# Query and key preparation inside the projections, and V multiplied with tokens on partitions

## The reference

```python
# even layer: part of the combined projection is attention with grouped heads
q, k, v = split(h @ w_in)            # 8 query heads, 2 key/value heads of 64
q, k = rms_norm(q, q_gain), rms_norm(k, k_gain)      # per head and token
ql, kl = apply_axial_rope(ql, cos, sin), apply_axial_rope(kl, cos, sin)   # latent tokens only
p = softmax(q . k * 64 ** -0.5); out = p @ v

# odd layer: differential attention, no norm of q and k
pl = hl @ w_in                       # q, k, v of 1024 columns each; q for latent tokens only
ql, kl = rope(ql), rope(kl)
p = softmax(q1 . k1 / 8) - lam * softmax(q2 . k2 / 8); out = p @ v
```

## Time and profile before

| what | value |
|---|---|
| time, median of 3 runs | 5691.41 us (5691.09 to 5696.93) |
| the profiled execution | 5694.67 us, its span 5692.4 us |
| PE busy | 4159.3 us, 73% |
| DVE busy | 2207.1 us, 39% |
| ACT busy | 1421.9 us, 25% |
| POOL busy | 638.5 us, 11% |

### The profile page before, as it was taken

The page is one execution under the profiler, slowest core; times in us unless marked ns, Lnnn a source line. Parts: engine busy times, 40 slices in busy tenths (PEclk is TensorE's granted clock), DMA queues, the critical chain, the costliest instruction groups (busy, mean ns, idle before and its releaser), DMA issues. The chain is left out here.

```text
span 5692.4 us, 71074 instructions
## 1 busy us (share of the span) xinstructions
PE 4159.3 (73%) x23474; PEld 2745.7 (48%) x23475; DVE 2207.1 (39%) x4258; ACT 1421.9 (25%) x3188; POOL 638.5 (11%) x1135
## 2 busy tenths in 40 slices
PE   5597499396794949756499994599189955499983
PEld 0386277285683848635133331488056644133321
DVE  0312644565656656543300002411767743300003
ACT  0211255343333424312011110210056632011111
POOL 0000100131322313310200002000300000100001
PEclk9798799698897979877699997699599977799996
DMA  9421100101001010034468897321520023357996
GB/s 334 150 88 66 71 10 8 41 1 25 10 1 34 1 34 1 25 122 141 179 253 307 353 398 294 134 83 66 190 78 10 10 87 122 156 221 316 396 427 232
DMA packets 210800, 778.83 MB, mean 137 GB/s; under 512 B 52000, under 2 KB 95285, under 8 KB 185957
## 3 DMA queue, kind: packets, MB, share of 16 engines
q1 hardware_dynamic: 158376, 624.64, 29.0%
q10 hardware_dynamic: 37696, 103.04, 4.7%
q0 software_dynamic: 14544, 48.79, 2.3%
HBM read 656.45 MB, written 122.58 MB: 137 GB/s over the span
## 5 line engine op out<-in xcount | busy, mean ns | idle before, releaser
L2305 PE MATMUL ex_bY<-ex_w,ex_aT 128*64 x880 | 390.9, 597 | 74.6 <-DVE ex_aT L2368 65.5
L2305 PE MATMUL ex_bG<-ex_w,ex_xT 128*64 x880 | 405.6, 616 | 41.0 <-SPq L2226 27.5
L2308 PE MATMUL ex_bG<-ex_w,ex_xT 128*64 128x512 f32 x880 | 405.6, 616 | 0.0
L367 PE MATMUL p_acc<-hT,p_wh 128*128 128x512 f32 (+1 forms) x1056 | 376.0, 356 | 24.7 <-DVE p_wl L379 24.7
L2308 PE MATMUL ex_bY<-ex_w,ex_aT 128*64 128x512 f32 x880 | 391.1, 597 | 0.0
L2305 PE MATMUL ex_bU<-ex_w,ex_xT 128*64 x880 | 386.6, 592 | 0.0
L2308 PE MATMUL ex_bU<-ex_w,ex_xT 128*64 128x512 f32 x880 | 386.6, 592 | 0.0
L367 PE MATMUL p_acc<-hT_rest,p_wh 128*128 128x512 f32 (+1 forms) x1056 | 375.8, 356 | 0.0
L367 PE MATMUL p_acc<-hT,p_wl 128*128 128x512 f32 (+1 forms) x1056 | 375.1, 355 | 0.0
L2366 DVE TENSOR_TENSOR ex_a<-ex_sg,ex_bU 128x512 f32<-128x512 f32 x55 | 37.8, 687 | 811.2 <-PE ex_bU L2308 811.2
L703 PE MATMUL ad_S<-ad_K,ad_q 64*128 64x512 f32 (+1 forms) x768 | 191.4, 577 | 125.7 <-DMA ad_lqk<-in_od_lk 120.6
(11 more groups left out here) (361 smaller groups left out, 8861.7 us busy)
## 6 DMA issues: line engine op xcount, KB each, us to landing
ex_w<-in_moe_w_gate SPq DMA_DIRECT2D x64, 2048.0 KB, 12.0
ex_w<-in_moe_w_up SPq DMA_DIRECT2D x64, 2048.0 KB, 16.0
ex_w<-in_moe_w_down SPq DMA_DIRECT2D x64, 2048.0 KB, 14.3
mods_w<-in_mod_w SPq DMA_DIRECT2D x24, 2048.0 KB, 13.1
projT_dram<-p_o ACTq DMA_DIRECT2D x44, 640.0 KB, 2.9
yb_dram<-ex_y ACTq DMA_DIRECT2D x55, 512.0 KB, 10.1
p_w<-in_od_w_in SPq DMA_DIRECT2D x12, 1024.0 KB, 5.1
n_x<-x_dram SPq DMA_DIRECT2D x20, 512.0 KB, 3.8
```

What stands on the lines that cost most here:

```text
L367: mm = nc.tensor.matmul(acc[u % 2][c][:, 0:n], a[:, u // 2, k, at], b[:, k, t0:t0 + n], start=k == 0 and x == 0, stop=k == KT - 1 and x == 2)
L2305: nc.tensor.matmul(bank[0:BR, :], stationary[:, k, 0:BR], w[:, ds(slot0 + (offset + k * n), 512)], start=k == 0, stop=k == tiles - 1)
L2308: m = nc.tensor.matmul(bank[BR:P, :], stationary[:, k, BR:P], w[:, at:at + 512], start=k == 0, stop=k == tiles - 1)
```

## The change

Both `qk_phase` stages are removed. The two projections get functions of their own.

In `even_proj_phase` tiles 0 to 3 are q, tile 4 is k, tile 5 is V and tiles 6 to 19 go to `projT` as before. For a q tile ACT squares the evacuated `o` and writes gain times `o` to `xn`; DVE and POOL rotate `xn`, and ACT stores it to `qT`. The sums of squares come from 10 matmuls of 2 columns, issued after chunk 0 of the next tile; their root and reciprocal (20 numbers per partition) are kept in `rq`. They are not applied to q: the first attention multiplies each row of scores by `rq` where it multiplied by 1.0. The k tile is normed in full, with the matmul against `blockones` after each chunk of tile 5, the long reciprocal, gain, rotation and store. Tile 5 (V) is transposed after the chunks of tile 6 and copied by ACT.

In `odd_proj_phase` q is computed for the 1024 latent tokens only (two chunks of 512) and rotated in `o`; k is rotated in `o` too. V is computed with tokens on partitions: for each 256 columns, 10 token tiles of 24 matmuls of 256 columns, evacuated by DVE and ACT in turn and stored to `v_dram`. The second attention loads V from there (10 loads of 512 KB, after the first K and q) and waits for all of it before its first product with V.

The diff, cut to its core:

```diff
-def proj_phase(nc, sems, tag, w_dram, hT, outT):
...
+def even_proj_phase(nc, sems, d, hT, projT, qT, kT, V, rq):
...
+    NQ, KEYS, VALS, PLAIN = AW // P, AW // P, AW // P + 1, A_COLS // P
...
+                def extras(g, c):
+                    if c == 0 and 1 <= g <= NQ:
+                        if g == 1:
+                            pe.wait_ge(const_in, C_IN)
+                        else:
+                            pe.wait_ge(sd_done, g - 1)
+                        pe.wait_ge(sq_done, g)
+                        for t in range(NT):
+                            x = nc.tensor.matmul(sums[:, 2 * t:2 * t + 2], sq[:, t * P:(t + 1) * P], hc[:, :], start=True, stop=True)
+                        x.then_inc(ss_done, 1)
+                    if g == KEYS + 1:
+                        pe.wait_ge(sq_done, NQ + 1)
+                        pe.wait_ge(sd_done, NQ + c)
+                        t0, n = TCH[c]
+                        nc.tensor.matmul(sums[:, 0:n], ones[:, :], sq[:, t0:t0 + n], start=True, stop=True).then_inc(ss_done, 1)
+                    if g == VALS + 1:
+                        pe.wait_ge(dve_ev, 4 + 2 * VALS + 2)
+                        pe.wait_ge(act_ev, 2 + VALS + 1)
+                        if c:
+                            pe.wait_ge(v_done, c)
+                        for t in range(4 * c, min(4 * c + 4, NT)):
+                            x = nc.tensor.transpose(tr[:, (t - 4 * c) * P:(t - 4 * c + 1) * P], o[:, VALS % 2, t * P:(t + 1) * P], ident[:, :])
+                        x.then_inc(tr_done, 1)
...
+                            extras(tile(i, u), c)
...
+                def rope(g):
+                    if g == 0:
+                        dve.wait_ge(const_in, C_IN)
+                    else:
+                        dve.wait_ge(rope_done, g)
+                    x = xn[:, g % 2, CTX:TOK]
+                    nc.vector.tensor_tensor(ra[:, :], x, cos[:, :], ALU.mult).then_inc(ra_done, 1)
+                    nc.vector.stream_shuffle(sh[:, :], x, SWAP16).then_inc(sh_done, 1)
+                    dve.wait_ge(ra_done, g + 1)
+                    dve.wait_ge(rb_done, g + 1)
+                    nc.vector.tensor_tensor(x, ra[:, :], sh[:, :], ALU.add).then_inc(rope_done, 1)
+                def queries(g):
+                    if g < NQ:
+                        dve.wait_ge(gained, g + 1)
+                        rope(g)
+                    if 1 <= g <= NQ:
+                        dve.wait_ge(sd_done, g)
+                        nc.vector.reciprocal(rq[:, :, 2 * (g - 1):2 * g], sd[:, :, :]).then_inc(rq_done, 1)
+                def keys():
+                    dve.wait_ge(sd_done, NQ + 3)
+                    nc.vector.reciprocal(rk[:, :], rk[:, :]).then_inc(kn_done, 1)
+                    dve.wait_ge(kn_done, 1)
+                    dve.wait_ge(x_out[KEYS % 2], 16 * (KEYS // 2))
+                    nc.vector.scalar_tensor_tensor(out=xn[:, KEYS % 2, :], in0=o[:, KEYS % 2, :], scalar=gain[:, 1:2], in1=rk[:, :], op0=ALU.mult, op1=ALU.mult).then_inc(kn_done, 1)
+                    dve.wait_ge(kn_done, 2)
+                    dve.sem_inc(o_out[KEYS % 2], 16)
+                    rope(KEYS)
...
+                def squares(g):
+                    if g:
+                        act.wait_ge(ss_done, g)
+                    nc.scalar.activation(sq[:, :], o[:, g % 2, :], ACT.Square).then_inc(sq_done, 1)
+                    if g < NQ:
+                        if g == 0:
+                            act.wait_ge(const_in, C_IN)
+                        if g >= 2:
+                            act.wait_ge(x_out[g % 2], 16 * (g // 2))
+                        nc.scalar.activation(xn[:, g % 2, :], o[:, g % 2, :], ACT.Copy, scale=gain[:, 0:1]).then_inc(gained, 1)
+                        act.wait_ge(sq_done, g + 1)
+                        act.wait_ge(gained, g + 1)
+                        act.sem_inc(o_out[g % 2], 16)
...
+                def query_sums(g):
+                    act.wait_ge(ss_done, g)
+                    if g >= 2:
+                        act.wait_ge(rq_done, g - 1)
+                    nc.scalar.activation(sd[:, :, :].rearrange("p t h -> p (t h)"), sums[:, 0:2 * NT], ACT.Sqrt, scale=1.0, bias=eps[:, 0:1]).then_inc(sd_done, 1)
...
+                        if g == VALS + 1:
+                            for c in range(NB):
+                                values(c)
+                            act.wait_ge(v_done, NB)
+                            act.sem_inc(o_out[VALS % 2], 16)
...
+                        if g <= KEYS:
+                            squares(g)
+                        if g >= PLAIN:
+                            act.dma_start(projT[ds(i * (U * P) + u * P, P), :], o[:, u % 2, :]).then_inc(o_out[u % 2], 16)
+                        if 1 <= g <= KEYS:
+                            store(g - 1)
+                        if g == VALS + 1:
+                            store(KEYS)
...
-def qk_phase(nc, sems, tag, d, projT, tiles, vrows, V, gains=None):
...
+def odd_proj_phase(nc, sems, d, hT, qT, kT, v_rows):
...
+    QCH = ((CTX, 512), (CTX + 512, 512))
+    NQ, NK = U * QI, U * (KI - QI)
...
+                with pe.Fori(0, QI) as i:
+                    tiles(i, QCH, lambda g: g + 1)
+                with pe.Fori(QI, KI) as i:
+                    tiles(i, TCH, lambda g: 2 * g - NQ + 1)
+                for i in range(KI, ITERS):
+                    for v in range(2):
+                        pe.wait_ge(rest_done, 2 * i + v + 1)
+                        for t in range(NT):
+                            n = 2 * NT * (i - KI) + NT * v + t
+                            if t % 2 == 0:
+                                pe.wait_ge(dve_ev, V_DVE + n // 2)
+                            if t % 2 == 1 or n == 0:
+                                pe.wait_ge(act_ev, V_ACT + n // 2)
+                            for k in range(KT):
+                                for x, (a, b) in enumerate(((lead, wh), (rest, wh), (lead, wl))):
+                                    mm = nc.tensor.matmul(acc[t % 2][0][:, 0:2 * P], a[:, k, t * P:(t + 1) * P], b[:, v, k, :],
+                                                          start=k == 0 and x == 0, stop=k == KT - 1 and x == 2)
+                            mm.then_inc(mm_done, 1)
...
+                def rope(i, u, evacuated):
+                    g = U * i + u
+                    x = o[:, u % 2, CTX:TOK]
+                    dve.wait_ge(dve_ev, evacuated)
+                    dve.wait_ge(act_ev, 2 + g + 1)
+                    nc.vector.tensor_tensor(ra[:, :], x, cos[:, :], ALU.mult).then_inc(ra_done, 1)
+                    nc.vector.stream_shuffle(sh[:, :], x, SWAP16).then_inc(sh_done, 1)
+                    dve.wait_ge(ra_done, g + 1)
+                    dve.wait_ge(rb_done, g + 1)
+                    nc.vector.tensor_tensor(x, ra[:, :], sh[:, :], ALU.add).then_inc(rope_done, 1)
+                    dve.wait_ge(rope_done, g + 1)
...
+                def queries(i):
+                    for u in range(U):
+                        dve.wait_ge(o_out[u % 2], 16 * (2 * i + u // 2 + 1))
+                        dve.wait_ge(mm_done, q_seen(i, u, 0))
+                        t0, n = QCH[0]
+                        nc.vector.tensor_scalar(o[:, u % 2, t0:t0 + n], acc[u % 2][0][:, 0:n], HD ** -0.5, None, ALU.mult).then_inc(dve_ev, 1)
+                        if u % 2 == 1:
+                            split(i + 1, u // 2)
+                        rope(i, u, 2 + U * i + u + 1)
...
+                def tiles(i, chunk, seen, last, scale, store):
+                    for u in range(U):
+                        act.wait_ge(o_out[u % 2], 16 * (2 * i + u // 2 + 1))
+                        t0, n = chunk
+                        act.wait_ge(mm_done, seen(i, u, 1))
+                        nc.scalar.activation(o[:, u % 2, t0:t0 + n], acc[u % 2][1][:, 0:n], ACT.Copy, scale=scale).then_inc(act_ev, 1)
+                        if u % 2 == 1:
+                            act.wait_ge(mm_done, seen(i, u, last))
+                            split(i + 1, u // 2)
+                        act.wait_ge(rope_done, U * i + u + 1)
+                        store(i, u)
...
+                            act.dma_start(v_rows[2 * a * P:(2 * a + 2) * P, c0:c0 + 2 * P].rearrange("(t p) c -> p t c", p=P), vo[:, e % 2, :, :]).then_inc(v_out[e % 2], 16)
...
-def gqa_qk(nc, sems, d, projT, qT, kT, V):
...
+                    if i == 0 and v_rows is not None:
+                        for t in range(NT):
+                            sp.dma_start(V[:, t, :], v_rows[t * P:(t + 1) * P, :]).then_inc(v_in, 16)
...
+                    if i == 0 and m == 0 and v_rows is not None:
+                        pe.wait_ge(v_in, 16 * NT)
...
-                        nc.vector.tensor_scalar(p[:, u, c, a:a + w], S[j % 2][c][:, 0:w], 1.0, None, ALU.mult, ALU.max, accum_out=top[:, u, c, i:i + 1]).then_inc(s_out, 1)
+                        pair, t, nk = units[n]
```

(75 more changed lines are left out.)

331 lines of the change are left out of this document (160 added, 171 removed).

## The result

The changed kernel takes 5435.24 us in the median (4 runs, 5430.37 to 5438.39), the one before 5692.83 us (4 runs). The ratio is 0.9545, 95% interval 0.9533 to 0.9557: 4.5% less. The forecast was 5434 us, 5420 to 5464. The profiled execution of the changed kernel took 5433.25 us, its span is 5431.4 us; against the 5692.4 us of the span before, 261.0 us are gone.

The account below looks back on a forecast made before the run. PE was taken to bound the projections, with DVE, ACT and POOL mostly idle there, but not the q/k stages. Terms summed to −257.9 us: 5694.7 profiled gave 5436.8, or 5434 us against the median; range 5420 to 5464.

Parts of the forecast that it names:

- Removed stages, odd q without context, odd V: Two q/k stages go, −267.4 us; eight odd q tiles lose their context chunk, −23.0; odd V by token tiles, +4.6.
- rival B: Odd V: weight loads no longer hidden when the operands' roles are swapped, +48 us, giving 5482; chance 0.05.
- rival D: Both projections: small pauses keep TensorE at half clock throughout, +517 us, about 5950; chance 0.01.
- Rotation at no cost: Odd layer: each rotation, a 6.2 us chain on DVE and POOL, hides beside PE within slack; cost 0.
- Rivals A: Odd q tiles: helpers become the bound if two-input steps take 3.24 us; 5465 us; chance 0.10.
- C: Some wait ties the next tile to the rotation before it, in 21 q/k tiles: +147 us, 5581; chance 0.04.
- Waits: PE waits: even k sums 1.6 us, V's second transposes 4.9; odd k to V 0.75, third V token tile 4.8.
- Query sums, +9.7: Even layer: PE's sums of squares for four q tiles, 20 small passes each at 0.12 us, +9.7 us.
- The upper end of +17.7: Even-layer query sums if each 20 passes run cold at 4.43 us: +17.7 us.
- Clock, +2.4: Half-clock start after each of the two new 5 us stalls: 0 to 4.8 us, half taken, +2.4.
- The pointer's 0: First attention: scores multiplied by a number from memory, 0.065 us more on each of 208, hidden: 0, up to +13.5.
- V's 0: Second attention: V loaded behind the first K and q lands before its first use: 0, up to +6 us.

Follow-up runs that it names:

- `even_only`: The changed kernel with the odd layer's functions as before, so only the even layer has the new form; 5589.70 us (ratio 0.9822).
- `sums_twice`: The changed kernel with each of the ten query-sum matmuls of an even-layer q tile issued twice, in one stretch; 5453.90 us (ratio 0.9585).

## Why the prediction was right, and where only in the sum

- **Removed stages, odd q without context, odd V** (−267.4, −23.0, +4.6). Held. The odd stage lost 157.0 us where the terms say 156.6. In the trace after, a q tile takes 10.9 us and V's token tiles have a pitch of 2.88 us, so rival B (weight loads that show, +48 us) didn't occur. The granted clock is 0.96 and 0.97 over the two projections, so rival D (half clock throughout) didn't either.
- **Rotation at no cost.** Held. The 16 chains of the odd layer, from the cos product to the end of the addition, took 6.24 to 6.31 us each (6.2 in the working), and DVE's products never took more than 1.23 us. The slack is measured too: one product of 1.2 us more on each rotation moves only the last tile, three break it. Rivals A (steps of 3.24 us) and C are out; C would have made the stage some 110 us longer.
- **Waits.** All four where the working put them and within 0.7 us; taking their causes away took three of them away.
- **Query sums, +9.7: a term mis-sized by what it left out.** The passes cost 4 × (274.83 − 272.69) = 8.6 us, 0.107 each where the earlier trace rows had 0.12. What the step put at nothing is what comes behind them: the stretch can be followed by half clock, which cost 1.68 us in the changed kernel, 10.3 with the passes. The upper end of +17.7 stood for cold passes, not for a cold time after them. The Trainium skill ("TensorE: Matmul & The Clock Gate", section "Wait — 56ns, not 53.3ns?") gives about 25 ns as the least start-to-start time of small matmuls; measured are 107 to 112 ns a pass where each has its own weight load, so as a price for this case the page's figure is too low, and the measurement decides.
- **Clock, +2.4: mis-sized by almost half.** The step took an even chance for each stall; both were followed by half clock. The windows view of the changed kernel around the first and the second:

```profile
366.40:372.00 5.60, 5.55 (x26) 0.50 0.00 0
372.00:380.00 8.00, 8.00 (x39) 1.00 0.76 213
...
3753.20:3756.00 2.80, 2.73 (x13) 0.50 0.84 325
3756.00:3759.00 3.00, 3.00 (x19) 0.66 0.01 3
3759.00:3762.00 3.00, 3.00 (x27) 1.00 0.00 0
```

  Behind the first, 22 matmuls of 256 columns took 372.02 − 367.19 = 4.83 us instead of 2.64: 2.2 lost; behind the second, 22 took 3758.09 − 3753.27 = 4.82 us, 2.2 again. So 4.4 us, and 6.1 with the sums' 1.7. (The 2.4 us were a cold start's; its 4.5 us at 0.43 us per matmul would be a loss of 2.1, while the start of the first projection in the trace before is 12 such matmuls, 5.3 us long with 2.5 lost.) The Trainium skill (same page, section "HAM oscillation — how this bites in real kernels") said that waits of this length each bring the clock back to half; the trace agrees for the two waits of 4.24 and 4.58 us, and I should have taken it whole. The wait of 1.42 us had no such effect.
- **Attentions.** The pointer's 0 is about 1 us. Of its upper bound, 13.5 us of DVE work, 12.3 were measured (0.059 us each; the two rows differ by 0.069, not the 0.065 of the working), and nearly all of it was hidden. V's 0 holds within what is measured (476.6 and 476.8 us).
- **The sum** of −257.9 against −257.6 between the medians is closer than its parts, and that is luck. The stages of the change lost 255.9 us between the traces, 2.0 less than forecast; the rest of the difference, 1.7 us between the medians and 5.1 between the traces, is that of stages whose code is the same. In the even layer the clock cost 2.7 us more than its share there (2.2 + 1.7 − 1.2), the sums 1.1 and the waits 0.8 less; in the odd layer the clock cost 1.0 more, the waits 0.7 less.

## What to carry to other kernels

Work can be moved beside a stage that one engine bounds, at a cost that can be counted beforehand: what the bounding engine gets more itself, and one wait at each place where a chain of the helpers ends within a tile. The order inside the helpers' queues decides these waits: evacuate what TensorE waits for ahead of what nobody needs soon, and spread small matmuls in short stretches among the dense ones. Price a wait of 4 to 5 us in front of dense matmuls at its length and some 2 us more.

## What the hardware showed that I had not expected

- The clock fell without any wait of TensorE. Behind small fp32 passes (2 columns, each with its own weight load) in one stretch of 4.5 us, matmuls of 512 columns went at 0.43 us for some 3 us in 4 cases of 4; behind 2.3 us in 8 of 28; behind 1.1 us in none of 40. The busy share shows nothing of it, PE is recorded busy throughout; only the granted clock and the matmuls' start-to-start times do.
- All twenty waits of TensorE between 4.16 and 10.26 us inside the projections of these traces were followed by half clock, at a loss of 1.4 to 2.9 us; those of 1.42 to 1.84 us were not. In `even_only` and `sums_twice` the matmuls behind the V tile's wait of 4.23 us first went at full clock for about 1 us and only then at half.
- In seven traces of unchanged sums it was always the third of the four stretches (once the fourth as well). Why the third is open. No run separates what it is about these passes, the few columns or the weight load of each.
- A scalar taken from memory in place of an immediate costs DVE 59 ns an instruction (748 against 689 ns for 512 columns, 481 against 422 for 256), alike at both lengths measured.
